# Rows of the experts' v table fetched alternately with the u rows, 32 rows behind

## The reference

```
q = (t @ wq).reshape(128, 8, 2, 128)                 # blocks of 128 tokens, 8 heads
v1, i1 = top_k(s1, 16); v2, i2 = top_k(s2, 16)       # s1, s2: q against two sets of 128 keys
score, ci = top_k(v1 + v2, 16)                       # 16 of 256 pairs
expert = i1[ci // 16] * 128 + i2[ci % 16]            # one of 16384 rows
g   = softmax(score)
act = gelu(einsum('thkd,td->thk', u_tab[expert], t)) # dot with a row of the u table
out = einsum('thk,thkd->td', g * act, v_tab[expert]) # weighted sum of rows of the v table
```

## Time and profile before

| what | value |
|---|---|
| device time, three runs | 4344.37, 4361.85, 4363.55 us (median 4361.85) |
| the profiled execution's own time | 4348.94 us |
| its span | 4347.0 us |
| busy share of the span | PE 83%, DVE 50%, POOL 28%, ACT 19% |
| L2591, 512 v rows (x2048 records) | 1031.1 us busy |
| L2668, 512 u rows | 622.5 us busy |
| gathers by POOL (L2638) | 1024, 559.2 us (u) and 557.5 us (v) busy |

### The profile page before, as it was taken

How to read it: one execution, slowest core, us unless ns; L and a number is a source line. 1 busy time by engine, 2 the same in 40 slices (tenths; PEclk the granted TensorE clock), 3 DMA queues, 4 the chain that set the end, 5 groups by cost and what they waited for, 6 DMA issues and landing times.

```text
span 4347.0 us, 33067 instructions
## 1 busy us (share of the span) xinstructions
PE 3596.0 (83%) x10942; PEld 1813.3 (42%) x10942; DVE 2153.0 (50%) x4711; ACT 845.3 (19%) x1796; POOL 1226.4 (28%) x1151
## 2 busy tenths in 40 slices
PE   8778998999997989939999974668776877776877
PEld 4334554444453564426644563334232333232322
DVE  0547523100013567966525448863686876433442
ACT  1224422000032221132211223011121221111111
POOL 0200000000000000000001013453787777777774
PEclk9876999999999989969999987889898998988988
DMA  3340021222211112200222256774999999999996
GB/s 152 138 150 1 1 97 49 77 77 77 97 58 49 63 54 104 76 34 34 75 76 97 104 196 214 258 248 160 385 338 348 342 365 359 355 370 369 353 377 263
DMA packets 171912, 765.16 MB, mean 176 GB/s; under 512 B 19256, under 2 KB 19256, under 8 KB 160224
## 3 DMA queue, kind: packets, MB, share of 16 engines
q0 software_dynamic: 157904, 580.06, 36.2%
q1 hardware_dynamic: 13824, 182.97, 11.5%
q10 hardware_dynamic: 16, 0.02, 0.0%
HBM read 744.08 MB, written 18.89 MB: 176 GB/s over the span
## 4 chain that ended last, share of the span: by engine, by line
PE 49%; DVE 20%; issue 8%; DMA 5%; POOL 4%; ACT 2%; another core or an unknown queue 1%; POOLq 0%; DVEq 0%; ACTq 0%
PE ps L252 13%; PE ps L258 9%; PE ps L2591 8%; DVE arena L2668 5%; PE ps L1327 5%; PE ps L1385 5%; DVE arena L1471 4%; POOL arena L2638 4%; DMA arena<-in_pu,arena 3%; PE ps L1609 2%; PE ps L220 2%; DMA arena<-in_pv,arena 2%; PE ps L1596 1%; PE ps L831 1%
## 5 line engine op out<-in xcount | busy, mean ns | idle before, releaser
L2591 PE MATMUL ps<-arena 128*128 128x512 f32 x2048 | 1031.1, 655 | 385.0 <-issue 163.9
L2591 PEld LDWEIGHTS ps<-arena 128*128 128x128 f32 x2048 | 404.9, 206 | 991.1 <-issue 786.8
L2668 DVE CUSTOM_DVE_ANT_0 arena<-arena 128x1024 f32<-128x1024 f32 x512 | 622.5, 1221 | 387.8 <-DMA arena<-in_pu,arena 350.2
L252 PE MATMUL ps<-arena 128*128 128x512 f32 (+1 forms) x1768 | 755.0, 587 | 31.5 <-ACT arena L2157 24.4
L2638 POOL DMA_INDIRECT arena<-in_pu,arena x512 | 559.2, 1092 | 419.8 <-issue 96.5
L2638 POOL DMA_INDIRECT arena<-in_pv,arena x512 | 557.5, 1089 | 196.3 <-issue 136.0
L258 PE MATMUL ps<-arena 128*128 128x512 f32 (+2 forms) x1408 | 527.7, 536 | 3.1 <-DVE arena L1300 0.9
L252 PEld LDWEIGHTS ps<-arena 128*128 128x128 f32 x1768 | 337.2, 192 | 434.8 <-issue 429.7
L258 PEld LDWEIGHTS ps<-arena 128*128 128x128 f32 x1408 | 268.2, 191 | 262.8 <-issue 220.4
L220 PE MATMUL ps<-arena 128*128 128x128 f32 (+1 forms) x1062 | 191.4, 314 | 203.0 <-ACT arena L1686 59.8
L263 POOL TENSOR_TENSOR arena<-arena 128x1 f32<-128x1 f32 (+7 forms) x38 | 61.4, 1617 | 1012.6 <-DVE arena L675 427.7
(11 more groups left out here) (334 smaller groups left out, 3120.8 us busy)
## 6 DMA issues: line engine op xcount, KB each, us to landing
arena<-in_w_in SPq DMA_DIRECT2D x27, 2048.0 KB, 9.6
arena<-in_w_ada SPq DMA_DIRECT2D x12, 2048.0 KB, 8.1
arena<-in_w_ff_in SPq DMA_DIRECT2D x8, 2048.0 KB, 7.8
arena<-in_w_ff_out SPq DMA_DIRECT2D x8, 2048.0 KB, 8.1
arena<-in_w_pq SPq DMA_DIRECT2D x8, 2048.0 KB, 8.1
aside<-arena POOLq DMA_DIRECT2D x20, 512.0 KB, 6.8
arena<-in_w_at SPq DMA_DIRECT2D x4, 2048.0 KB, 8.4
arena<-in_w_o SPq DMA_DIRECT2D x4, 2048.0 KB, 8.0
```

Source lines behind the costliest of these rows:

```text
L252: x = t.matmul(PS[:, b, 0:n], hT[:, k, i * 128:(i + 1) * 128], w[:, k, :], start=k == 0, stop=k == nk - 1)
L2591: x = t.matmul(PS[:, b + c, :], DG[n % 4], row(f)[:, 512 * c:512 * c + 512], start=j == 0, stop=j == 127)
L2668: v.tensor_tensor_reduce(row(f), row(f), TT[i], 1.0, 0.0, ALU.mult, ALU.add, DOT[i % 2][:, j:j + 1]).then_inc(*pe.V.step("dot", 128 * i + j))
```

## The change

The list is built by another rule: from u row 33 on one v row follows each u row, 32 rows behind it, to the end; the 33 v rows left then follow the last u row. `FROM`, where the ring grows from 7 places to 19, goes from gather 144 to gather 164. The `LATE` loads hang at v row 80 of tile 0 instead of 24. Nothing else is edited; all waits are derived from the list.

```diff
@@ -2385,11 +2385,12 @@
         BL = 16
+        BEHIND = 32
         FETCH = []
         done_v = 0
         for n_ in range(1, 513):
             FETCH.append(("pu", (n_ - 1) // 128, (n_ - 1) % 128))
-            goal = 0 if n_ < 64 else (n_ - 64) // 4 if n_ < 128 else 16 + (n_ - 128) * 5 // 4 if n_ < 512 else 512
+            goal = n_ - BEHIND if n_ < 512 else 512
             while done_v < goal:
                 FETCH.append(("pv", done_v // 128, done_v % 128))
                 done_v += 1
@@ -2398,7 +2399,7 @@
         MANY = len(PLACES)
-        FROM = 144
+        FROM = 164
         SPOT = [n % FEW if n < FROM else (n - FROM) % MANY for n in range(ROWS)]
@@ -2641,7 +2642,7 @@
             for f in in_order(g, tail_gpsimd, select, gather):
-                if f == ("pv", 0, 24):
+                if f == ("pv", 0, 80):
```

## The result

The changed kernel took 4378.74 us (median of 8 runs, 4372.59 to 4389.3), the kernel before beside it 4351.57 (8 runs, 4335.31 to 4363.55): ratio 1.0071, 95% interval [1.0051, 1.009], 27 us slower. The profiled execution took 4389.3 us, its span is 4387.5.

What follows compares the result with a forecast made beforehand. Taken as bound by DVE and PE by stages until the queries end, then by gather bytes. +41 - 29.6 + 0 + 5 = +16.5 us: 4365 by the profiled execution, 4378 by the median; middle 4372, range 4352 to 4390.

Steps and rivals of the forecast that it cites:

- The last query ends at about 3075, +41: Sum over the six stages before the ring opens, from 2676 us: the queries end 41 us later.
- S6, +25: 2915 to 3034 us, 16 query steps, PE-bound: 8.95 us per query period with more v rows, +25 us.
- S2, +19: Up to 2770 us, six `mm_tok` filling PE: nine v rows add their time and some waits, +19 us.
- S1, -5: 2676 to 2725 us, DVE-bound: eight dots fewer, half of their time saved, -5 us.
- S3, -3: 2770 to 2812 us, DVE-bound: five dots fewer, but v rows at 3.75 us nearly fill PE, -3 us.
- The rule weighed: Skill's warning that long waits before matmul bursts lower PE's clock; speaks against v rows strewn thinly through 2770 to 2915 us.
- The third rival: v rows at the low clock, each behind a wait, 3.75 us between 2770 and 2915 us: +67, 4416 us; chance 20%.
- S4, 0: 2812 to 2887 us, with the norms: five more v rows fit PE's idle time in a chain through DVE, 0 us.
- S5, +5: 2887 to 2915 us, no engine full: nine v rows and transposes need 24 to 40 us of PE, +5 us.
- 20 gathers more, -29.6: At the ring's opening: 20 more gathers already out, each worth 1.478 us of the DMA-bound stretch, -29.6 us.
- The DMA regime, 0: After the ring opens, 845 gathers bound by bytes: same bytes, so no change, 0 us (bounds -15, +15).
- The end, +5: After the last u row: 33 v rows instead of 16, PE slower than the gathers, +5 us.

Runs made afterwards that it cites:

- the halved matmul: Changed kernel, but v rows 1 to 68 of tile 0 do only the first of two matmuls: 1.0037 of the kernel before.
- the halved dot: Changed kernel, but dots of u rows 33 to 101 of tile 0 take 512 of 1024 features: 1.0095 of the kernel before.
- the head alone: Changed kernel's order only up to u row 128, then the lag shrinks evenly from 32 to 16 rows: 1.006 of the kernel before.
- the second and the third trace: The changed kernel run again twice without edit: 4383.65 us, 1.0055 of the kernel before, then 4303.0 us, 1.0085, on a faster chip.

## Why the prediction held, step by step

The time (4378.74) lies in the own range of the forecast (4352 to 4390), and the sum of +16.5 us stands against +27 by the medians and +29 by the traces. The direction and the two regimes were right. That the time came so near is in part luck: the price of the last query and the credit for 20 gathers were both too large and cancel, and the DMA regime's +8.3 us were not in the sum.

- *The last query ends at about 3075, +41.* Measured +34.9 from gather 0. PE's time as the main price is shown by the halved matmul, DVE's small part by the halved dot. The stages below are cut at the first matmul of each group; the earlier trace rows, on which I worked, has S3 and S5 begin 3 us too early.
- *S6, +25:* measured +24, period by period as computed.
- *S2, +19:* +11. The nine v rows took 16.7 us, 1.8 a row, and cost next to no turn-around. But one stood there before too (2.0 us), and the six blocks themselves ran 3.5 us shorter, at a granted clock of 1.00 instead of 0.95.
- *S1, -5:* +1. I called S1 DVE's. DVE had 10 us less to do (32.2 us busy for 42.1) and the stage did not shorten; in all 14 traces S2 starts 134.0 to 136.8 us after gather 0, with half dots as well. What bounds S1 was not tried.
- *S3, -3:* -9. Here I was wrong by the clock: I took the v rows at 3.75 us. Their 37 records took 18.34 us, 2.0 a row, at a granted clock of 0.94; the three before took 11.3 us, 3.8 a row, each behind a wait, at 0.65.
- *The rule weighed.* The warning of the Trainium skill ("TensorE: Matmul & The Clock Gate", section "Loop structure matters more than you think") fits the kernel before better than the changed one: S1, S3 and S5 went from 0.60, 0.67 and 0.76 to 0.80, 0.94 and 0.96. What is left of it are the three v rows of S4 that stand 5.21 us behind an idle PE: they still take 3.6 to 3.75 us. The third rival, built on the low clock for all rows, is out.
- *S4, 0:* +2. I named the chain through DVE's norm but not its link: the diagonal behind the square on ACT. I also took S4's idle PE time for room. Part of it was made by the v rows themselves: with none among the projection's matmuls the stage is 17 us shorter (61.4 for 78.4), and PE idles 15 us in it instead of 23; with nine of them it is 83.8. Four rows cost nearly as much as nine, so the change added little here.
- *S5, +5:* +5 (29.5 for 24.2).
- *20 gathers more, -29.6:* mis-sized. The gather-200 line gives a net of +13.0, and +34.9 - 13.0 = 21.9 us, about 15 gathers. I counted issued gathers as landed. Before, POOL had stood 26 us and all 159 gathers had landed. In the changed kernel 178 were out, but 14 of them were issued only after the wait of gather 164, and from there to the query's end the DMA engines moved 5.37 MB, 10.2 gathers: some 174 had landed, 15 more than before. That this wait comes from the choice of `FROM` I did not see. Net +13.0 against the +11.5 of the sum: two errors that cancel.
- *The DMA regime, 0:* +8.3 after gather 200, the one term that I called nothing. Its cause is open, and strict alternation is not shown to be it. On the slower chips the orders near five to four took 1219.4, 1223.6 and 1226.2 us from gather 200 to 1023, strict alternation 1227.7 and 1228.2, the head alone, nearly the same order, 1238.2. On the faster chips there is no difference: 1150.4 to 1158.7 against 1148.6 to 1160.8.
- *The end, +5:* +7.9 between the two traces and 3 to 8 over all pairs of the table, so the term holds: PE, at 1.79 us a row, is slower than the gathers at 1.49.

## What to carry to other kernels

A row of work costs what its engine lacks at that place. One v row was about 2 us among matmuls that fill PE (S2, S6) and next to nothing in S1, where PE waited for another engine; in S4, where its operand is made by an engine that stands behind a long wait, four rows were worth 17 us. So ask of each place what stands ahead of the row on every engine that it touches, before you read idle time as room. When an order ends one phase and feeds another, count what has landed at the hand-over, not what was issued. And where a ring of buffers changes its size, look how far back the last user of the first place is.

## What the runs showed of the hardware

- The pace of the gathers differs by 6% from chip to chip: in the changed kernel, gathers 200 to 1000 took 1.492 and 1.494 us each on the first chips and 1.406 on another. The DMA regime of the second and the third trace, in that order:

```profile
3071.00:4334.00 1263.00, 879.89 (x1782) 354.38 (x1783) 769.17 (x1867) 205.97 (x541) 938.90 (x857) 0.88 0.96 356
```
```profile
3072.00:4258.00 1186.00, 863.42 (x1799) 330.92 (x1800) 771.63 (x1866) 207.87 (x543) 914.42 (x856) 0.94 0.99 379
```

- In that regime, on the slower chips, ACT now and then stands for 8 to 23 us with everything that the profile shows as its wait long done, and PE and DVE stop behind it. The longest, in the changed kernel: PE's matmuls for this copy had ended at 3523.65.

```profile
3543.73 0.60 ACT L2473 ACTIVATE arena<-ps 128x512 f32<-128x512 f32 x1 [23.07 <-remote]
```

It cost POOL a wait of 9.75 us; the 19 places hid the rest. The kernel before has such a stop of 19.66 us too. Each of the six traces of the slower chips has 11 to 14 waits of ACT of 8 us and more behind 3080 us that the profile puts down to "issue" or "remote"; the eight traces of the faster chips have none. So the stops and the slower pace go together; which causes which, or whether both have another cause, was not tried.
